# Hybrid convolution layer on eight cores: longer runs for the shifted copies, later bulk loads, and eight tile transposes moved to the DMA engines

## The reference, cut to what matters

```python
h = rmsnorm(x, norm_mix_g)
a_val, a_gate, b_gate, c_gate, b_in = split(h @ w_in)            # 5 x 512 columns
u  = a_val * sigmoid(a_gate)
ua = causal depthwise conv, width 31 (u) + bias
ya = beta_a * silu(per-head LayerNorm(ua))
z  = c_gate * b_in
yb = beta_b * b_gate * causal depthwise conv, width 3 (z)
x  = x + concat(ya, yb) @ w_out
h  = rmsnorm(x, norm_ffn_g);  up = h @ w_up                      # 1024 -> 5632
x  = x + (silu(conv3(up)_gate) * conv3(up)_val) @ w_down         # 2816 -> 1024
y  = rmsnorm(x, norm_final_g)
```

## Time and profile before

| | |
|---|---|
| runs, us | 798.91, 801.19 and 915.09; median 801.19 |
| the profiled execution, us | 799.11 |
| its longest span, us (core 7) | 797.6 |
| spans of the other cores, us | 793.1 to 795.5 |
| PE, DVE, ACT, POOL busy on core 7 | 97%, 70%, 52%, 27% |
| granted TensorE clock, mean of a core | 0.994 to 0.999 |
| stage 1, 2, 3 on core 7 | to about 307 us, to about 629 us, to 797.6 us |

### The profile page before, as it was taken

How to read it: one execution, slowest core, us unless ns; L and a number is a source line. 1 busy time by engine, 2 the same in 40 slices (tenths; PEclk the granted TensorE clock), 3 DMA queues, 4 the chain that set the end, 5 groups by cost and what they waited for, 6 DMA issues and landing times.

```text
span 797.6 us, 15231 instructions; the slowest of 8 cores (793.1 to 797.6 us)
## 1 busy us (share of the span) xinstructions
PE 770.9 (97%) x5048; PEld 404.1 (51%) x5048; DVE 559.5 (70%) x633; ACT 411.8 (52%) x651; POOL 213.3 (27%) x281
## 2 busy tenths in 40 slices
PE   5998999999999999999999999999999999999996
PEld 3665556555565644445444445445445444444443
DVE  4555597867686887789999999999999805233323
ACT  5455778595856567555555555555556403111112
POOL 7002021103141401354434434434434400000000
PEclk9999999999999999999999999999999999999999
DMA  8999742633685862321311322312212454532211
GB/s 180 166 219 188 204 154 90 176 133 82 172 183 176 161 191 111 47 46 31 59 32 31 58 33 33 57 32 37 52 29 45 90 163 116 201 106 106 83 73 57
DMA packets 40324, 83.82 MB, mean 105 GB/s; under 512 B 10131, under 2 KB 22931, under 8 KB 40102
## 3 DMA queue, kind: packets, MB, share of 16 engines
q1 hardware_dynamic: 32324, 53.59, 22.7%
q0 software_dynamic: 7488, 28.84, 21.1%
q10 hardware_dynamic: 434, 0.42, 0.2%
HBM read 80.90 MB, written 19.71 MB: 126 GB/s over the span
## 4 chain that ended last, share of the span: by engine, by line
PE 89%; DVE 3%; issue 3%; ACT 2%; DMA 2%; POOL 1%; DVEq 0%; ACTq 0%; POOLq 0%
PE ps L1103 37%; PE ps L1311 19%; PE ps L678 18%; PE ps L846 6%; PE ps L733 3%; PE ps L1143 3%; ACT arena L502 2%; DMA arena<-xp 2%; PE ps L646 1%; PE ps L1335 1%; DVE arena L506 1%; DVE arena L518 1%; DVE arena L511 1%; PE ps L748 1%; PE ps L755 1%
## 5 line engine op out<-in xcount | busy, mean ns | idle before, releaser
L1103 PE MATMUL ps<-arena 128*128 128x512 bf16 x1408 | 308.5, 378 | 0.7 <-ACT arena L502 0.4
L502 ACT ACTIVATE arena<-arena 128x168 f32<-128x168 f32 (+8 forms) x222 | 155.1, 704 | 234.4 <-DVE arena L511 132.3
L506 DVE SCALAR_TENSOR_TENSOR arena<-ps,arena 128x1020 f32<-128x1020 f32 (+2 forms) x200 | 234.4, 1191 | 17.8 <-ACT arena L502 9.0
L1103 PEld LDWEIGHTS ps<-arena 128*128 128x128 bf16 x1408 | 135.0, 97 | 163.2 <-issue 1.4
L506 DVE SCALAR_TENSOR_TENSOR arena<-arena 128x168 f32<-128x168 f32 (+11 forms) x217 | 187.6, 871 | 36.8 <-POOL arena L800 17.7
L678 PE MATMUL ps<-arena 128*128 128x384 bf16 (+1 forms) x960 | 158.6, 323 | 7.2 <-ACT arena L502 4.1
L1311 PE MATMUL ps<-arena 128*128 128x512 bf16 x704 | 152.1, 379 | 0.0
L511 POOL TENSOR_TENSOR arena<-arena 128x1020 bf16<-128x1020 f32 (+2 forms) x88 | 118.1, 1343 | 112.9 <-DVE arena L506 86.9
L502 ACT ACTIVATE arena<-ps,arena 128x1020 f32<-128x1020 f32 (+2 forms) x112 | 109.4, 986 | 52.4 <-PE ps L1103 51.2
L511 DVE TENSOR_TENSOR arena<-ps,arena 128x512 f32<-128x512 f32 (+4 forms) x99 | 60.9, 618 | 93.5 <-PE ps L1311 81.9
L678 PEld LDWEIGHTS ps<-arena 128*128 128x128 bf16 x960 | 92.1, 99 | 64.9 <-issue 13.6
(11 more groups left out here) (47 smaller groups left out, 249.5 us busy)
## 6 DMA issues: line engine op xcount, KB each, us to landing
arena<-xp SPq DMA_DIRECT2D x26, 512.0 KB, 7.0
arena<-wup POOLq DMA_DIRECT2D x22, 512.0 KB, 7.0
x2d<-arena SPq DMA_DIRECT2D x17, 512.0 KB, 3.2
arena<-x2d SPq DMA_DIRECT2D x17, 512.0 KB, 6.2
yp<-arena SPq DMA_DIRECT2D x15, 512.0 KB, 2.7
arena<-arena SPq DMA_DIRECT2D x64, 97.8 KB, 2.3
arena<-wdn POOLq DMA_DIRECT2D x11, 512.0 KB, 5.4
arena<-xp POOLq DMA_DIRECT2D x6, 512.0 KB, 21.8
```

The source lines that it names most:

```text
L502: P.add("act", lambda e: e.activation(out=out, in_=in_, func=func, **kw), reads=reads, writes=writes, after=after, c=c - 60.0, table=TABLE ...
L506: P.add("dve", lambda e: e.scalar_tensor_tensor(out=out, in0=in0, scalar=scalar, in1=in1, op0=op0, op1=op1), reads=reads, writes=writes, c ...
L1103: ins = e.matmul(ps[:, b, :], lhsT=wv[:, k, 128 * gv:128 * gv + 128], rhs=h2T[:, k, c0:c0 + 512], start=(k == 0), stop=(k == 7))
```

## The change

Four things change in stage 1; stages 2 and 3 differ only in a column offset (h2T's columns begin at 14 instead of 0).

1. **Long runs.** U4, U4b and ub get one row pitch (UW, 416 columns), so that spread copies one run of 1664 columns (3328 bytes) for each of 32 partitions, where it copied four runs of up to 391 columns (782 bytes). It is still 16 DMAs for a chunk. The cost that the scheduler sees for such a DMA falls from 820 to 450 ns and its bytes are halved.
2. **Bulk loads later.** The four loads of w_out, and gb2, zs_h and the first loads of xo, wait for the last copy of spread(1) (V4_33) instead of spread(0) (U4_33).
3. **Roots by tile** in chunk 1: a root of ACT and a reciprocal of DVE after each sq1(1, t) instead of one for all three. In chunks 0 and 1 the copy out of PSUM behind a transpose moves from ACT to DVE.
4. **Turns.** For eight tiles, T1(4, 0..2), T2(0, 1..2) and T2(1, 0..2), the eight TensorE transposes and the copy are replaced by one transposing DMA issued from SP (turn). Up to iteration 3 three hn buffers are used in turn instead of two; the third lies in a part of h2T that is not written yet, as does junk, the unused output of the squares.

```diff
@@ layout
-    U4W = CW + 8
-    o = A.take(16 * U4W * 2)
-    U4 = A.bf16(o, 16 * U4W).rearrange("p (g n) -> p g n", g=16)
+    UF = 4 * UW + 24
+    o = A.take(16 * UW * 2)
+    U4 = A.bf16(o, 16 * UW).rearrange("p (q c n) -> p q c n", q=4, c=4)
-    U4b = A.bf16(o_h2 + 12288, 16 * U4W).rearrange("p (g n) -> p g n", g=16)
+    U4b = h2T[:, 3:7, 0:4 * UW].rearrange("p q (c n) -> p q c n", c=4)
+    junk = h2T[:, :, H2W - 128:H2W]
+    hn.append(h2T[:, 7, HN3:HN3 + D])
@@ dma
-        nb = out.shape[0] * fsz(out) * 4
+        nb = out.shape[0] * fsz(out) * (2 if pool == "u4" else 4)
-                     dma=f"{pool}{i % n}", c=600.0 if eng == "pool" else (820.0 if pool == "u4" else 450.0), nbytes=nb, name=f"dma {pool}")
+                     dma=f"{pool}{i % n}", c=600.0 if eng == "pool" else 450.0, nbytes=nb, name=f"dma {pool}")
@@ trans, turn, T1, T2
-        act(out, pv[:, :, 0:nt], AF.Copy, [f"ps{b}"], [okey])
+        if dve:
+            cp("dve", out, pv[:, :, 0:nt], [f"ps{b}"], [okey])
+        else:
+            act(out, pv[:, :, 0:nt], AF.Copy, [f"ps{b}"], [okey])
+
+    def turn(h, nt, out, okey):
+        P.add("sp", lambda e: e.dma_start_transpose(out=out, in_=hn[h][0:nt, :]), reads=[f"hn{h}"], writes=[okey],
+              dma=f"tr{h}_", c=600.0, nbytes=nt * 5400, name="turn")
-        trans(hn_of[(1, i, t)], nt, hT[i % 2][:, :, col:col + nt], f"hT{i % 2}_{t}")
+        if i == 4:
+            turn(hn_of[(1, i, t)], nt, hT[i % 2][:, :, col:col + nt], f"hT{i % 2}_{t}")
+            return
+        trans(hn_of[(1, i, t)], nt, hT[i % 2][:, :, col:col + nt], f"hT{i % 2}_{t}", dve=(i < 2))
-        trans(hn_of[(2, i, t)], nt, h2T[:, :, h:h + nt], f"h2_{i}_{t}")
+        f = turn if i < 2 and nt == 128 else trans
+        f(hn_of[(2, i, t)], nt, h2T[:, :, h:h + nt], f"h2_{i}_{t}")
@@ spread
-                dma("sp", U[32 * s:32 * s + 32, q:16:4, 0:n], ub[p][32 * q:32 * q + 32, :, 8 * s:8 * s + n],
+                dma("sp", U[32 * s:32 * s + 32, q].rearrange("p c n -> p (c n)"), ubf[p][32 * q:32 * q + 32, 8 * s:8 * s + 4 * UW],
@@ load_xo, w_out, roots
-        dma("sp", xo[s][0:nt, :], x_src(kind, row, nt), writes=[f"xo{s}"], pool=f"xo{s}_", n=1, after=["U4_33"])
+        dma("sp", xo[s][0:nt, :], x_src(kind, row, nt), writes=[f"xo{s}"], pool=f"xo{s}_", n=1, after=["V4_33" if i == 0 else "U4_33"])
-    root(st1, 0, 3, "st1")
+        root(st1, t, t + 1, "st1")
-    for q in range(4):
-        dma("pool", w_out[:, 2 * q:2 * q + 2, :].rearrange("p k n -> p (k n)"), wout[q], writes=[f"wo{q}"], pool="wo", n=4,
-            after=["U4_33"])
+        if i == 0:
+            for q in range(4):
+                dma("pool", w_out[:, 2 * q:2 * q + 2, :].rearrange("p k n -> p (k n)"), wout[q], writes=[f"wo{q}"], pool="wo", n=4,
+                    after=["V4_33"])
     for i in range(NCH - 1):
+        hn_n["ring"] = 3 if i < 4 else 2
```

More of the change, by code:

```diff
@@ L823, in otiles @@
             if kind == "m":
[L824 removed]
+                out.append((kind, 14, 2, row, 14))
             else:
[L826 removed]
+                out.append((kind, col, nt, row, 16 + (SEQ + row if kind == "s" else row)))
         return out
```

55 lines of the change are left out of this document (27 added, 28 removed).

## The result

The changed kernel takes 804.9 us (median of 9 runs, 803.3 to 808.0) against 799.4 us for the kernel before on the same chip: ratio **1.007** [1.005, 1.009] (in brackets the 95% interval). It is slower by 0.7%, which lies within the 2% of the class that was forecast, but 14 us above the 790.9 of the prediction and outside its range, which ended at 800.5.

The account below looks back on a forecast made before the run. TensorE's own work (PE busy 97%) was taken as the bound; 797.6 - 3.6 - 0.9 - 0.6 - 1.0 - 2.1 = 789.4 us of span, with 1.5 us around it 790.9 us; range 785.5 to 800.5.

Parts of the forecast that it names:

- The turns: no wait: Before stA(4, 0): three transposing DMAs should land in 11.0 us, inside 13.4, so TensorE would not wait.
- The window of 13.4 us: Time for the three turns of T1(4), from hT free at 147.7 us to stA(4, 0) at 161.1.
- 3 x 2.9 + 2.3 = 11.0: Three turns at 2.9 us each on SP plus 2.3 us to landing, the time expected before stA(4, 0).
- T: Time one turn takes up SP and the DMA engines: taken as 2.9 us, bounds 1.9 and 5.6.
- the rival of turns that come moderately late: At 5.6 us a turn, TensorE waits 5.7 us before stA(4, 0): 797.5 us in all; chance 0.15.
- The rival in which they hold SP: Each turn holds SP's queue as long as a whole spread, 11.2 us: 832 us in all; chance 0.08.
- 3.6 + 0.9 + 0.6 = 5.1 us for turns, center wait and start: Gains: 64 matmuls removed 3.6 us, waits around center and stA(4, 0) 0.9, earlier start of chunk 1 0.6.
- "a lighter spread(0)": TensorE's gaps of 1.25 and 0.73 us behind late loads of x(2) would halve, gaining 1.0 us.
- Spread's issue falling to 0.4 us: On SP, long runs would cut issue from 0.70 to about 0.4 us a DMA, 11.2 to 6 or 8 a spread.
- Bulk loads later, -2.1 us: The stall at 66 us would go, counting 2.1 us; w0B up to 3 us late, taken up by DVE.
- The rival that POOL is held: Spread(1) lands late, w0B comes 12 to 14 us late, some 8 us lost: 799 us; chance 0.10.
- I start from 795.5: With core 7's stall gone, the next two cores at 795.5 us set the time, counting 2.1 us.

Follow-up runs that it names:

- e6: Changed kernel with spread(0) in old short pieces, iteration 4's root back in place and bulk loads back behind spread(0): 795.6 us, ratio 0.999 to the kernel before.
- e18: e16 with spread in long runs for chunks 1 to 5, order worked out anew: 797.7 us, ratio 0.9985 to the kernel before.
- e16: Kernel before with turns, roots by tile and DVE's copies, POOL's 128x4096 multiplication moved back near its old time: 793.8 us, ratio 0.994.
- e9: e7 with the roots by tile and the copies of chunks 0 and 1 on DVE: 798.0 us, ratio 0.999 to the kernel before.
- e7: Kernel before with the turns alone, with the hn buffers and layout they need: 798.8 us, ratio 1.001 to the kernel before.
- e1: Changed kernel with spread(0) alone back in the old short pieces of 279 columns, same order: 798.8 us, ratio 1.003 to the kernel before.
- e2: Changed kernel with spread(0) in short pieces of 391 columns, nearly the long runs' bytes: 803.0 us, ratio 1.008 to the kernel before.
- e15: e9 with POOL's multiplication and one ACT square of iteration 4 moved later, spread(0) in pieces of 391 columns: 801.2 us, ratio 1.004 to the kernel before.
- e5: Changed kernel with spread(0) in old short pieces and iteration 4's root behind the center's squares: 797.0 us, ratio 0.999 to the kernel before.
- e17: e16 with all the bulk loads put later, behind spread(1), order worked out anew: 802.0 us, ratio 1.004 to the kernel before.
- e4: Changed kernel without turns, transposes and copies back, two hn buffers, order worked out anew: 805.5 us, ratio 1.011 to the kernel before.

## Why the prediction was wrong, step by step

- **The turns: no wait, as forecast, but by a wrong window and some luck.** The window of 13.4 us began at 147.7 us, when hT is free. But the three turns stand behind spread(3) on SP, whose issue has until 150.2, and they start at 153.7. From there to stA(4, 0) are 9.2 us, and 3 x 2.9 + 2.3 = 11.0 would have been 1.8 us late. They were in time because the three take 5.0 us of SP, so T is 1.7, under the lower bound of 1.9, though a turn lands in 3.1 to 7.4 us instead of 2.3. In e6 and e18, where the first two take 7.1 us together (core 2) and the third stands behind one more load of x, PE waits up to 3.6 us: the rival of turns that come moderately late exists, by what stands among them, not by their own price. The rival in which they hold SP is excluded, and by that the Trainium skill's 32 cycles for each 256 bytes ("DMA: Bandwidth & Descriptors", the comparison with previous generations; an estimated 27 us for a turn) does not hold here: on core 7 a turn takes SP 1.38 us at the median and 3.74 at most.
- **3.6 + 0.9 + 0.6 = 5.1 us for turns, center wait and start: about right in sum, for the parts by themselves.** e16, which has these and the old places of all else, is 0.6% or 4.8 us faster. The turns were sized too high: from conv(2, 0) to conv(4, 0), where all eight transposes and the center wait lie, seven of its cores gain 2.9 to 3.2 us and one 2.2, not 4.5. The roots and DVE's copies are some 0.2% (e9 against e7), not separated from nothing by the intervals; PE then waits for wina instead (0.70 and 0.57 us on core 7 of the changed kernel), a wait that the sum did not have. Where the rest of the 4.8 us comes from is open.
- **51 to 53 us, "a lighter spread(0)", -1.0 us: the step that failed first**, in sign, and the one that cost most. Fewer, longer runs were taken as less work for the DMA engines. They are more bytes in each packet at DMA engines that were already full (95.9 and 6.9% of their time for the two queues before), and it is the neighbour that pays: 5.1 us more in this gap on core 7, and eight matmuls at half clock behind it. Short pieces alone bring it back (e1), with nearly the same bytes too (e2, e15).
- **Spread's issue falling to 0.4 us: wrong.** The changed spread of chunks 1 to 5 is issued in 10.2 to 12.9 us over the eight cores, 0.64 to 0.80 us for each DMA, where it was 0.67 to 0.78. The 0.33 us of a load of x was the wrong neighbour: the row it should have been read from is the same kind of move, SBUF to SBUF on 32 partitions.
- **Bulk loads later, -2.1 us: the stall went, and the wait that replaced it was undersized.** The stall of 3.05 us at 66 us did go, on every core, which gave the changed kernel's core 7 its 52.5 in the second row of the table. But w0B comes at 74.1, 7.3 us later than before, not up to 3: with the loads of x(2) late, spread(1) starts at 59.3 us instead of 54.8 and has landed only at 71.9. DVE did not take that up: conv(0, 2) to conv(2, 0) is 1.7 to 4.8 us longer in the changed kernel, and in e5, where all comes sooner, 4 to 10. The first reader of w_out was not asked for at all. In the changed kernel that costs nothing; in e17's order its 2 MB are needed at 94 us and PE waits. The rival that POOL is held, at +8 us, was the nearest of those written down; it had 0.10.
- **The order of the other lists: not costed.** Two instructions that the diff does not name, the root of iteration 4 on ACT and the 128x4096 multiplication on POOL, changed places because the planner's times moved. The sum had no term for it, though the order of the changed kernel was there to be read. They cost 1.4 us on core 7 and 5.5 on core 4 between conv(4, 0) and conv(5, 0), of which the root is 1.4 to 3.1 (the seven cores that the multiplication does not touch). In e9, where POOL also stands waiting for the multiplication's load, its place costs 0.5% (e9 against e16, intervals apart).
- **The metric, "I start from 795.5": one execution read as a property of a core.** Core 7 was 2.1 us behind in the profiled execution alone. In the 12 executions of the kernel before beside e1 to e4 each of the eight cores is the slowest at least once, and the median span of every core lies between 792.8 and 793.3 us. So there was no core to relieve: a stall of this kind hits now one core and now another, and the time is that of the worst of eight. A loss of some us on one of them counts in full; a gain counts only if all have it.

The forecast's own list of what would prove it wrong names the third place (w0B later than 70 us; PE waiting for a DMA) but neither of the two that cost most: ahead of 55 us, and near 210 us, PE waits for ACT. What stays open is the last 0.2% of e15, and what e5, at 0.999, lacks to the 0.990 of the forecast: the wait of POOL for spread(1) is the largest piece that the traces show.

## What to carry to other kernels

When DMA engines are full, ask of a transfer that is made faster who shares them and whose deadline comes first; a transfer nobody waits for should not be made faster while others beside it are waited for. When a cost that a scheduler sees is changed, compare the whole order of every engine and cost each long instruction that moved, in the diff or not. Before a load is put off, find its first reader as well as what stands behind it in its queue. And before one core's delay is counted as a gain, look at the spans of several executions: the slowest core may be another each time.
